# Border blocks of query columns attend over 24 key columns, and VectorE alternates copies with pairs of biases

## The reference, cut to what matters

```python
win_start = np.clip(q_col - NA_WIN_W // 2, 0, GRID_W - NA_WIN_W)
k_start = np.clip(blk * NA_QBLK - NA_WIN_W // 2, 0, GRID_W - NA_KBLK)
valid = (kk >= ws) & (kk < ws + NA_WIN_W)
bias_c = jnp.where(valid, bias_c, -jnp.inf)
s = jnp.einsum('bhnqd,bhrnkd->bhnqrk', q_b, k_blk) + bias
p = softmax(s); o = jnp.einsum('bhnqrk,bhrnkd->bhnqd', p, v_blk)
```

## Time and profile before

| | us |
|---|---|
| median of 3 runs | 3317.02 (3315.56 to 3318.46) |
| the profiled execution, its own time | 3313.79 |
| its span, first to last instruction | 3312.0 |
| first score of the attention stage | 2160.9 |
| last value of the attention stage | 2761.4 to about 2762 |
| PE busy over the whole span | 3173.5 (96%) |
| DVE, ACT, POOL busy over the whole span | 1509.1, 867.6, 492.6 |

### The profile page before, as it was taken

The page is one execution under the profiler, slowest core; times in us unless marked ns, Lnnn a source line. Parts: engine busy times, 40 slices in busy tenths (PEclk is TensorE's granted clock), DMA queues, the critical chain, the costliest instruction groups (busy, mean ns, idle before and its releaser), DMA issues. The chain is left out here.

```text
span 3312.0 us, 50037 instructions
## 1 busy us (share of the span) xinstructions
PE 3173.5 (96%) x17152; PEld 2681.4 (81%) x17152; DVE 1509.1 (46%) x3180; ACT 867.6 (26%) x1832; POOL 492.6 (15%) x462
## 2 busy tenths in 40 slices
PE   5999999999998999999999999889999997999999
PEld 1777788888886888888888888778898886888887
DVE  2433433334335333333333333345555565777775
ACT  2222223323223111111111111145555552111110
POOL 0111111111111000000000000022223221333332
PEclk8999999999999999999999999989999998999999
DMA  7367554555545222222222222187578644656554
GB/s 289 126 204 263 164 161 157 160 184 166 160 148 174 82 80 81 81 84 82 78 78 78 78 78 78 67 261 188 141 208 254 166 122 137 203 203 208 198 204 144
DMA packets 232177, 498.34 MB, mean 150 GB/s; under 512 B 27604, under 2 KB 102356, under 8 KB 227670
## 3 DMA queue, kind: packets, MB, share of 16 engines
q1 hardware_dynamic: 230968, 493.46, 46.8%
q0 software_dynamic: 1152, 4.19, 0.4%
HBM read 311.36 MB, written 195.65 MB: 153 GB/s over the span
## 5 line engine op out<-in xcount | busy, mean ns | idle before, releaser
L287 PE MATMUL proj<-w_att_hi,a_h_hi 128*128 128x512 f32 x2560 | 1027.9, 402 | 23.3 <-DVE a_h_lo L389 13.6
L287 PE MATMUL proj<-w_att_hi,a_h_lo 128*128 128x512 f32 x2560 | 1003.5, 392 | 0.0
L287 PE MATMUL proj<-w_att_lo,a_h_hi 128*128 128x512 f32 x2560 | 1002.6, 392 | 0.0
L287 PEld LDWEIGHTS proj<-w_att_hi,a_h_hi 128*128 128x128 f32 x2560 | 484.5, 189 | 117.6 <-issue 14.6
L287 PEld LDWEIGHTS proj<-w_att_hi,a_h_lo 128*128 128x128 f32 x2560 | 483.5, 189 | 104.1
L287 PEld LDWEIGHTS proj<-w_att_lo,a_h_hi 128*128 128x128 f32 x2560 | 484.9, 189 | 93.0
L1286 PE MATMUL o_bank<-v_strip,probs_T 120*128 120x64 f32 x2560 | 330.0, 272 | 18.9 <-DVE probs_T L1206 13.1
L1286 PEld LDWEIGHTS o_bank<-v_strip,probs_T 120*128 120x128 f32 x2560 | 311.7, 192 | 38.0 <-DVE probs_T L1206 33.4
L1137 POOL CAST q_block<-q_strip 128x512 fp32r<-128x512 f32 x80 | 48.8, 610 | 1521.2 <-DMA q_strip<-qT_d 1106.2
L1579 PE MATMUL o_proj<-w_out_hi,o_m_hi 128*128 128x512 f32 x640 | 256.7, 401 | 2.5 <-DVE o_m_lo L1500 2.5
L1579 PE MATMUL o_proj<-w_out_hi,o_m_lo 128*128 128x512 f32 x640 | 253.1, 395 | 0.0
(11 more groups left out here) (130 smaller groups left out, 3567.8 us busy)
## 6 DMA issues: line engine op xcount, KB each, us to landing
k_strip<-kT_d SPq DMA_DIRECT2D x20, 1920.0 KB, 11.1
a_x<-in_x SPq DMA_DIRECT2D x40, 512.0 KB, 4.8
a_xT<-in_xT SPq DMA_DIRECT2D x40, 512.0 KB, 5.6
h_d<-a_h_hi SPq DMA_DIRECT2D x40, 512.0 KB, 2.7
h_d<-a_h_lo SPq DMA_DIRECT2D x40, 512.0 KB, 3.6
kT_d<-k_parts SPq DMA_DIRECT2D x80, 256.0 KB, 4.7
q_strip<-qT_d SPq DMA_DIRECT2D x40, 512.0 KB, 7.0
o_x<-in_x SPq DMA_DIRECT2D x40, 512.0 KB, 3.7
```

The costliest lines, as they stand in the source:

```text
L287: last = self.nc.tensor.matmul(bank, h[:, par, k, :], w[:, k, cols], start=(k == 0 and j == 0), stop=(k == KB - 1 and j == 2))
```

## The change

Blocks 0 and 3 of every strip take 24 key columns in place of 32, so 15 x 24 = 360 keys and 3 chunks. The last block starts at column 40 in place of 32, and reads its bias table from column 8 on. Tables, loads of keys and values, and semaphore counts stay as they are. Since the rows of a table still hold 32 columns, the border biases read 15 runs of 24 elements there; scores and biased scores are packed as 15 rows of 24.

On DVE the copies are placed differently: a unit's list was four biases and two copies, and is now two biases, copy, two biases, copy.

```diff
-K0 = [0, 8, 24, 32]
+K0 = [0, 8, 24, 40]
+KCS = [24, 32, 32, 24]
+TABLE_C0 = [0, 0, 0, 8]
...
-                nc.scalar.activation(probs[:, j % 4].rearrange("p (c r w) -> p c r w", r=KR, w=8),
-                                     biased[:, j % 4].rearrange("p (r c w) -> p c r w", r=KR, w=8), ACT.Exp, scale=-1.0,
+                width = KR * KCS[j // GH % COLS]
+                nc.scalar.activation(probs[:, j % 4, 0:width].rearrange("p (c r w) -> p c r w", r=KR, w=8),
+                                     biased[:, j % 4, 0:width].rearrange("p (r c w) -> p c r w", r=KR, w=8),
+                                     ACT.Exp, scale=-1.0,
...
-                nc.scalar.activation(probs_T[0:GROUP_KEYS, 0].rearrange("p c q -> p (c q)"),
-                                     t_banks[0][0:GROUP_KEYS].rearrange("p c q -> p (c q)"),
+                chunks = KCS[j // GH % COLS] // 8
+                nc.scalar.activation(probs_T[0:GROUP_KEYS, 0, 0:chunks].rearrange("p c q -> p (c q)"),
+                                     t_banks[0][0:GROUP_KEYS, 0:chunks].rearrange("p c q -> p (c q)"),
...
-                nc.vector.tensor_tensor_reduce(out=biased[:, j % 4, :], in0=s_banks[j % 4][:, 0:KEYS],
-                                               in1=tables[:, slot, KIND[j // GH % COLS], j % GH, :], scale=1.0,
-                                               scalar=3.0e38, op0=ALU.add, op1=ALU.min,
+                n = j // GH % COLS
+                rows = lambda ap: ap.rearrange("p (r k) -> p r k", r=KR)
+                bias = rows(tables[:, slot, KIND[n], j % GH, :])[:, :, TABLE_C0[n]:TABLE_C0[n] + KCS[n]]
+                nc.vector.tensor_tensor_reduce(out=rows(biased[:, j % 4, 0:KR * KCS[n]]),
+                                               in0=rows(s_banks[j % 4][:, 0:KR * KCS[n]]),
+                                               in1=bias, scale=1.0, scalar=3.0e38, op0=ALU.add, op1=ALU.min,
...
-                nc.vector.tensor_copy(probs_T[0:GROUP_KEYS, 1], t_banks[1][0:GROUP_KEYS]).then_inc(turned_dve, 1)
+                chunks = KCS[j // GH % COLS] // 8
+                nc.vector.tensor_copy(probs_T[0:GROUP_KEYS, 1, 0:chunks],
+                                      t_banks[1][0:GROUP_KEYS, 0:chunks]).then_inc(turned_dve, 1)
...
                     for h in range(GH):
                         add_bias(b, slot, GH * u + h)
-                    if not (first and u == 0):
-                        take_out(b, GH * u - 3)
-                        take_out(b, GH * u - 1)
+                        if h % 2 == 1 and not (first and u == 0):
+                            take_out(b, GH * u + h - GH)
                     if not (first and u < 2):
                         scale_unit(b, u - 2)
...
-                    last = nc.tensor.matmul(s_banks[j % 4][:, 0:KEYS], q_block[:, u % 2, part, h, :],
-                                            keys[:, :, k0:k0 + KC], start=(part == 0), stop=(part == 1))
+                    last = nc.tensor.matmul(s_banks[j % 4][:, 0:KR * kc], q_block[:, u % 2, part, h, :],
+                                            keys[:, :, k0:k0 + kc], start=(part == 0), stop=(part == 1))
...
-                for c in range(4):
+                for c in range(KCS[j // GH % COLS] // 8):
                     last = nc.tensor.transpose(t_banks[j % 2][0:GROUP_KEYS, c, :],
...
-                for c in range(4):
+                chunks = KCS[u % COLS] // 8
+                for c in range(chunks):
                     last = nc.tensor.matmul(o_banks[u % 2][:, cols], probs_T[0:GROUP_KEYS, j % 2, c, :],
                                             v_strip[0:GROUP_KEYS, u // COLS, K0[u % COLS] // 8 + c, cols],
-                                            start=(c == 0), stop=(c == 3))
+                                            start=(c == 0), stop=(c == chunks - 1))
```

More of the change, by code:

```diff
@@ L1261, in score @@
                 keys = k_strip[:, u // COLS, h, :].rearrange("p (r w) -> p r w", w=W)
-                k0 = K0[u % COLS]
+                k0, kc = K0[u % COLS], KCS[u % COLS]
                 for part in range(2):
-                    last = nc.tensor.matmul(s_banks[j % 4][:, 0:KEYS], q_block[:, u % 2, part, h, :],
-                                            keys[:, :, k0:k0 + KC], start=(part == 0), stop=(part == 1))
+                    last = nc.tensor.matmul(s_banks[j % 4][:, 0:KR * kc], q_block[:, u % 2, part, h, :],
+                                            keys[:, :, k0:k0 + kc], start=(part == 0), stop=(part == 1))
                 last.then_inc(scored, 1)
```

## The result

The changed kernel takes 3209.44 us (median of 4 runs, 3207.24 to 3211.7) against 3316.32 us: the ratio is 0.968 with a 95% interval of 0.966 to 0.969. A second set of runs gave 3210.99 against 3315.59 us. The forecast was 3220, its range 3211 to 3240. So the sign and the mechanism held, and the gain was 107 us (105 in the second set) where 97 was forecast.

The account below looks back on a forecast made before the run. PE was taken to bound the attention stage. Fewer columns (65.5 us) plus the removed DVE queue (33.4) less 2 for thin cover gave 96.9 us, so 3216.9 from the profiled execution and 3220 as median; range 3211 to 3240.

Parts of the forecast that it names:

- queue on DVE: Value's second weight load waits for a DVE copy standing behind four biases, 0.43 us per unit; moving the copy saves 33.4 us.
- score term: Border units' eight score matmuls shrink from 480 to 360 columns, 50 ns less each, 0.40 us per unit; bounds 0.21 and 0.44.
- part 1: Fewer columns on PE in border units: transposes, values and scores save 1.68 us per unit, 65.5 us over 39 units.
- late copies: Copies in border units, with 0.03 to 0.04 us spare, might make PE wait; 2 us taken off the gain for it.
- values: Value passes in border units fall from eight to six per step at 0.105 us each, saving 0.84 us per unit.
- turns: One transpose fewer per step in border units, 0.11 us each over four steps, saving 0.44 us per unit.
- rival 2: Border scores don't shrink by ticks but by 26 ns per matmul: 7 us less gain, 3228 us; chance 0.08.
- The page's rule: Skill page's matmul spacing, 81 ns at 128 columns and 131 at 512: 16 ns saved per score matmul, 0.12 us per unit.
- The chains: From a turn's first transpose load to value in border units: 1.25 us on DVE, 1.26 on ACT, against PE's cover of 1.29.
- Rival 1: Border units are bound by the copies, 0.1 us late three times a unit: 12 us, 3230 us; chance 0.20.
- Rival 3: The queue only changes place and PE waits elsewhere for the 0.43 us: 33 us stay, 3253 us; chance 0.10.
- Rival 4: Slower kernel: a border bias pays for each of its 15 runs, needing 1.58 us for a 6.6 us loss; chance 0.02.

Follow-up runs that it names:

- one_run: The changed kernel with the keys of every score taken as one run of 360 or 480 columns in place of 15 runs of 24 or 32: 3208.27 us.

## Why the prediction was wrong, point by point

The mechanism was right: PE bounds the stage, half of its units lose some 1.7 us of PE's own work each, and the queue on DVE goes. The sizes of the sum were too small. The step that failed most is the score term of part 1, which chose 50 ns less per matmul where 58 were measured. Next come the queue's price and the 2 us taken off for late copies. From the fourth unit on, with the terms as each was measured by itself (late copies as the list of waits has them):

| term, us | forecast | measured |
|---|---|---|
| scores | 15.6 | 18.2 |
| values | 32.8 | 33.6 |
| turns | 17.2 | 16.3 |
| queue on DVE | 33.4 | 34.9 |
| late copies | -2.0 | -0.7 |
| not in these terms | | 1.5 |
| sum, before rounding | 96.9 | 103.8 |

- **What bounds the stage**: right. PE did, and does; the order alone removed PE's one wait.
- **The scores**: 2.6 us too little. The forecast chose ticks (50 ns) over proportion (55 ns), though its own bound named the latter. The starts of 360 columns lie 0.165 us apart, about three quarters of 0.22 (rival 2 had them shrink less than by ticks; they shrank more); 480 columns in 15 runs carry some 6 ns that 360 don't. The last 2 ns of the 58 were not traced. The lower end, 26 ns by a line through 480 and 512, was far off in part for the reason that the forecast gave, that one size has runs and the other none: with 480 columns in one run the same line gives (0.227 - 0.215)/32 x 120, so 45 ns. The page's rule that was weighed (the Trainium skill, "TensorE: Matmul & The Clock Gate", "Back-to-back issue gap") would have made the term 5 us, as an estimate; the undone term was 18.2. The trace does not bear out its sustained spacing.
- **Late copies**: 1.3 us too much taken off. The chains held, and PE's waits for copies are 0.7 us in all. Rival 1 was right in the price of a wait (0.10 us late, 60 times, cost 6.0 us), but its condition did not come about: 0.03 to 0.04 us were spare on DVE, as worked out.
- **The queue's price**: 1.5 us too little, because the bracket of a row (0.43 us) is less than what the starts lose (0.46).
- **The values**: 0.8 us too little. 0.105 us a pass came from starts of eight passes; taking two away from each step removed 33.6/312 = 0.108 a pass.
- **The turns**: 0.9 us too much.
- **Rival 3** did not come about: no wait of 0.4 us per unit stands on any line of PE. **Rival 4** did not either: a border bias takes 0.53 us, where 1.58 would have been needed. The Trainium skill, "Vector Engine (DVE) Microarchitecture Reference", section 5.2, says that a port keeps its full rate while its elements come in runs of two or more adjacent words that start on an 8-byte boundary, and that any hop between such runs is free. The trace agrees: 0.125 us less for 120 elements.
- **The first unit**: the forecast counted 39 units because PE waits for loads in the first. The first three units were in fact 1.0 and 1.4 us slower than before, which takes the 103.8 us to 102.6 for the stage.
- **The range**: its low end allowed 3.6 us for scores at 55 ns and no late copy, and 4 us for reading the starts. The stage gained 5.7 us more than the sum (102.6 against 96.9), and that alone would have given 3214, inside the range. The medians gained 4.0 and 2.2 us more than the stage did in each set's profile (106.9 against 102.9, 104.6 against 102.4), and the range held nothing for that: the time outside the stage differs by 4.7 us between executions of programs that are the same there, and the forecast had seen one profile and three runs. That the first median fell outside and the second on the edge is thus in part chance.

## What to carry to other kernels

Where one engine is busy throughout a stage, a change of its instruction counts can be priced by distances between starts and checked term by term, by putting each back alone; the durations of single pipelined instructions, which overlap, are of no use for it. When the bound engine's steps shrink, its cover for the others shrinks with them, so a queue on a half-idle engine grows dearer (here from 35 to 40 us): shorten and reorder together. Compare terms on a part of the stage that repeats: two profiles of one kernel agreed within 0.04 us from the fourth unit on, and differed by 0.4 us in the first three. A range must hold the error of every term in both directions, the ones that look exact too, and the scatter of the stages that aren't touched.

## What the runs showed of the hardware that was not expected

Keys read in 15 runs cost a score of 480 columns some 6 ns over one run (one_run: eight scores in 1.98 us in place of 2.03), and a score of 360 columns nothing measurable. The starts then lie some 14 to 15 ns further apart than the columns at 2.4 GHz alone: 0.215 us for 480 in one run (0.200), 0.165 for 360 (0.150), and 0.227 for 512 (0.213).
